# Banded attention units placed between the second pair of forgetting heads' units, their bias table in a raw weight buffer, blocks from the last down

## What is computed

```python
# forgetting attention, head by head, 128 queries at a time
logits = q @ k.T * scale + F[q] - F[k];  causal mask;  p = softmax(logits);  y_f = p @ v
# sliding window of 128, 2 key heads for 4 query heads: a block of 128 queries
# sees 256 keys (its own block and the one before)
logits = q @ band(k).T * scale - slope * dist;  mask dist outside 0..127
p = softmax(concat([logits, sink]))[..., :-1];  y_s = p @ band(v)
```

## Time and profile before

| | us |
|---|---|
| median of 3 runs | 1837.4 (1834.18 to 1841.05) |
| profiled execution | 1835.78 |
| its span on the core | 1834.0 |
| PE busy | 1742.1 (95%) |
| VectorE busy | 888.7 (48%) |
| ScalarE busy | 592.0 (32%) |
| GpSimd busy | 647.1 (35%) |

### The profile page before, as it was taken

The page is one execution under the profiler, slowest core; times in us unless marked ns, Lnnn a source line. Parts: engine busy times, 40 slices in busy tenths (PEclk is TensorE's granted clock), DMA queues, the critical chain, the costliest instruction groups (busy, mean ns, idle before and its releaser), DMA issues.

```text
span 1834.0 us, 22463 instructions
## 1 busy us (share of the span) xinstructions
PE 1742.1 (95%) x8340; PEld 1454.7 (79%) x8340; DVE 888.7 (48%) x1576; ACT 592.0 (32%) x965; POOL 647.1 (35%) x363
## 2 busy tenths in 40 slices
PE   2999999999999999899999979999999999999996
PEld 2887878877888888797887768888888888888885
DVE  5615646469999999275754252221122122022116
ACT  2434234472232222364334473212122112211213
POOL 0521221004356565401884444224214322321424
PEclk9999999998999999999999989999999999999998
DMA  8121131011111111503764212112102111111202
GB/s 302 57 82 45 59 96 39 9 50 32 54 43 54 46 43 63 166 1 137 284 203 161 81 35 69 35 46 65 49 23 69 57 34 46 57 34 46 69 23 92
DMA packets 36292, 135.58 MB, mean 74 GB/s; under 512 B 4496, under 2 KB 4496, under 8 KB 36240
## 3 DMA queue, kind: packets, MB, share of 16 engines
q1 hardware_dynamic: 34000, 127.55, 20.6%
q0 software_dynamic: 2240, 7.34, 1.9%
HBM read 118.62 MB, written 9.96 MB: 70 GB/s over the span
## 4 chain that ended last, share of the span: by engine, by line
PE 89%; DVE 5%; ACT 3%; DMA 2%; issue 1%; POOL 1%; SPq 0%; DVEq 0%; ACTq 0%
PE ps L484 26%; PE ps L486 26%; PE ps L485 26%; PE ps L673 4%; PE ps L652 2%; PE ps L578 1%; PE ps L579 1%; DMA region_b<-in_w_ada 1%; DVE region_a L1569 1%; DVE h_t L1535 1%; ACT y_t L873 1%; ACT region_d L1030 0%; PE ps L684 0%; PE ps L504 0%; DVE region_a L1583 0%
## 5 line engine op out<-in xcount | busy, mean ns | idle before, releaser
L484 PE MATMUL ps<-h_t,w_t 128*128 128x512 f32 x1632 | 640.6, 392 | 6.1 <-POOL w_t L1107 2.4
L485 PE MATMUL ps<-h_t,w_t 128*128 128x512 f32 x1632 | 637.6, 391 | 0.0
L486 PE MATMUL ps<-h_t,w_t 128*128 128x512 f32 x1632 | 637.3, 391 | 0.0
L484 PEld LDWEIGHTS ps<-h_t,w_t 128*128 128x128 f32 x1632 | 308.0, 189 | 73.6 <-issue 4.0
L486 PEld LDWEIGHTS ps<-h_t,w_t 128*128 128x128 f32 x1632 | 307.8, 189 | 64.5
L485 PEld LDWEIGHTS ps<-h_t,w_t 128*128 128x128 f32 x1632 | 308.1, 189 | 64.1 <-issue 0.5
L1107 POOL TENSOR_TENSOR w_t<-raw,w_t 128x1280 fp32r<-128x1280 f32 (+1 forms) x67 | 183.2, 2734 | 251.3 <-ACT w_t L833 161.1
L1578 DVE TENSOR_TENSOR region_d<-ps,region_d 128x512 f32<-128x512 f32 x44 | 30.4, 692 | 439.8 <-PE ps L486 439.8
L1583 DVE TENSOR_TENSOR region_a<-ps,region_a 128x512 f32<-128x512 f32 x176 | 121.1, 691 | 109.5 <-PE ps L486 109.5
L1344 DVE MAX8 top<-region_b 128x8 f32<-128x384 f32 (+5 forms) x192 | 157.9, 882 | 17.3 <-issue 16.7
L1347 DVE MATCH_REPLACE8 region_b<-top,region_b 128x384 f32<-128x384 f32 (+5 forms) x192 | 166.1, 876 | 0.0
(11 more groups left out here) (184 smaller groups left out, 2182.2 us busy)
## 6 DMA issues: line engine op xcount, KB each, us to landing
raw<-in_w_ffn SPq DMA_DIRECT2D x66, 512.0 KB, 3.5
region_b<-in_w_ada SPq DMA_DIRECT2D x48, 512.0 KB, 4.4
raw<-in_w_gates SPq DMA_DIRECT2D x32, 640.0 KB, 3.9
raw<-in_w_z SPq DMA_DIRECT2D x18, 512.0 KB, 3.3
raw<-in_w_o SPq DMA_DIRECT2D x16, 512.0 KB, 3.6
region_a<-in_x SPq DMA_DIRECT2D x8, 512.0 KB, 11.7
mix_dram<-region_a SPq DMA_DIRECT2D x8, 512.0 KB, 6.0
region_a<-mix_dram SPq DMA_DIRECT2D x8, 512.0 KB, 6.6
```

The costliest lines, as they stand in the source:

```text
L484: pe.matmul(o, a_hi, m_hi, start=first, stop=False)
L485: pe.matmul(o, a_hi, m_lo, start=False, stop=False)
L486: return pe.matmul(o, a_lo, m_hi, start=False, stop=last)
```

## The change

The second call of `attention` keeps its 24 units but in another order: after the two forgetting units of block b comes the banded unit of block b+1, and at the very end the banded unit of block 0. So the sequence is f7 f7 f6 f6 s7 f5 f5 s6 f4 f4 s5 f3 f3 s4 f2 f2 s3 f1 f1 s2 f0 f0 s1 s0. A banded block must follow the forgetting block of the same number, since its result overwrites part of the forgetting bias; an assertion says so. Group numbers are now counted from the order of the units. The bias table goes to `raw[:, 1]`, the buffer of tile 17, and tile 17 is loaded after the last unit's reduction. `ya_back` is read back after the last forgetting logits.

```diff
+        def fox_unit_pair(pair, b):
+            return [("fox", b, 2 * pair + j) for j in range(2)]
+
+        first_units = [u for b in reversed(range(TT)) for u in fox_unit_pair(0, b)]
+        second_units = [u for b in reversed(range(TT))
+                        for u in fox_unit_pair(1, b) + ([("swa", b + 1, None)] if b < TT - 1 else [])]
+        second_units.append(("swa", 0, None))
         dsa_units = [("dsa", b, h) for b in reversed(range(TT)) for h in range(HEADS)]
-        units = fox_units + swa_units + dsa_units
+        units = first_units + second_units + dsa_units
+        fox_end = 1 + max(u for u, (kind, b, h) in enumerate(units) if kind == "fox")
+        window_at = raw[:, 1, 0:L]
...
-            for j in range(2):
-                tile_load(T_AFS + j, w_gates[j])
-            sp.wait_ge(s_logit, U_SWA)
-            sp.dma_start(region_d[:, :], window_bias).then_inc(s_table, 16)
-            sp.wait_ge(s_of, O_SWA)
+            tile_load(T_AFS, w_gates[0])
+            sp.wait_ge(s_w_lo, T_AFS)
+            sp.dma_start(window_at, window_bias).then_inc(s_table, 16)
+            sp.wait_ge(s_logit, fox_end)
             sp.wait_ge(s_ya_out, 16 * BT)
             for ch in range(BT):
                 sp.dma_start(ya_back[:, ch], ya_dram[:, ch, :]).then_inc(s_ya_in, 16)
+            sp.wait_ge(s_lg, U_DSA)
+            tile_load(T_AFS + 1, w_gates[1])
...
-                            window_cols(region_d[:, :], b)[:, hh], 1.0, TAKEN, ALU.add, ALU.max,
+                            window_cols(window_at, b)[:, hh], 1.0, TAKEN, ALU.add, ALU.max,
```

More of the change, by code:

```diff
@@ L66 @@
 FFN_AHEAD = ((1,), (2, 3), (4, 5), (6,))
-U_FOX, U_SWA, U_DSA = 0, HEADS * TT, HEADS * TT + TT
-O_FOX, O_SWA, O_DSA = 0, 2 * TT, 3 * TT
+U_FOX, U_DSA = 0, HEADS * TT + TT
+O_DSA = 3 * TT
 MIX0 = 1
@@ L307, in build, with groups_split @@
         act_order = sem("act_order")
-        fox_units = [("fox", b, 2 * pair + j) for pair in range(2) for b in reversed(range(TT)) for j in range(2)]
-        swa_units = [("swa", b, None) for b in range(TT)]
-        dsa_units = [("dsa", b, h) for b in reversed(range(TT)) for h in range(HEADS)]
-        units = fox_units + swa_units + dsa_units
+        def fox_unit_pair(pair, b):
[4 more added lines that the diff above has]
+        second_units.append(("swa", 0, None))
+        dsa_units = [("dsa", b, h) for b in reversed(range(TT)) for h in range(HEADS)]
+        units = first_units + second_units + dsa_units
+        first_swa = min(u for u, (kind, b, h) in enumerate(units) if kind == "swa")
+        fox_end = 1 + max(u for u, (kind, b, h) in enumerate(units) if kind == "fox")
+        window_at = raw[:, 1, 0:L]
+        ends = [kind == "swa" or h in ((1, 3) if kind == "fox" else (HEADS - 1,)) for kind, b, h in units]
+        def groups_split(u):
+            return sum(end and kind != "swa" for end, (kind, b, h) in zip(ends[:u + 1], units))
         def group_of(u):
             kind, b, h = units[u]
[L319 to L323, removed]
+            n = {"fox": 2, "swa": 1, "dsa": HEADS}[kind]
+            j = (h or 0) % n
+            return ends[:u].count(True), j == 0, j == n - 1
         def group_bank(u):
@@ L365, in stack_scale @@
             return HD ** -0.5 if stacks[T][0] == "q" and T >= T_FOX else 1.0
+        assert all(units.index(("swa", b, None)) > units.index(("fox", b, 3)) for b in range(TT))
         def stack_parts(T):
@@ L1448, in group_lo @@
                 else:
-                    dve.wait_ge(s_o_hi, (g if kind == "fox" else g - TT) + 1)
+                    dve.wait_ge(s_o_hi, groups_split(u))
                     dst, src = group_turned(u, y_lo(1))
@@ L1462, in biased @@
                 if kind == "swa":
-                    if u == U_SWA:
+                    if u == first_swa:
                         dve.wait_ge(s_table, 16)
```

## The result

The changed kernel takes 1841.62 us (median of 12 runs, 1836.62 to 1846.3) against 1837.4 us before (12 runs, 1834.06 to 1841.05): ratio 1.0025, 95% interval 1.0014 to 1.0035. The two medians differ by 4.2 us; the ratio says some 4.6 us, with an interval of 2.6 to 6.4 us: slower, clear of noise but inside the half per cent band that the forecast called no change. The forecast was 1842.7 us. Its profiled execution took 1841.77 us, with a span of 1840.0 us (before: 1835.78 and 1834.0).

A forecast was written before the change was run, and what follows sets the result against it. TensorE (PE), busy 95%, was taken as the bound. Idle or lost time goes from 9.6 to 15.8 us (2.9 + 12.9), +6.2, less 0.9 for the gates: net +5.3, median 1842.7 us, range 1833 to 1849 us.

The forecast's parts named there:

- rival A: Tail before the gates keeps full clock, block 1's `den` addition gets in before POOL: +2 us, 1839.4 us; chance 0.20.
- the hole: 2.06 us PE gap where the second pair's banded units start, blamed on the bias table's late DMA.
- The price of 4.7 us: Gain from loading the table early: 2.06 us idle, 1.7 us clock loss and 0.96 us pipeline filling at the banded start.
- Tile 17 and `ya_back`: Their moved loads before the gates cost nothing; tile 17 uncovered would cost up to 4 us.
- The order: In the interleaved units PE waits 0.1, 0.5, 1.05, 1.25 us at blocks 4 to 1: 2.9 us, bounds 0 to 5.
- The tail up to the last transposition: Block 1's banded transposition at 4.8 us, the last at 7.65, with 1.5 and 1.65 us of PE idle.
- time 0: The prediction's mark for the tail: end of the transposition of the second-last forgetting unit (block 0, head 2).
- The clock in the tail: PE falls to half clock at about 7.65 us, making the tail 21.2 us, 12.9 idle or lost, instead of 17.6.
- the second shut-out: In the tail, block 1's `den` addition on DVE misses POOL's start at 11.3 us and waits until 15.8 us.
- The 0.9 us taken off for the gates: Half clock begins earlier, so less of it falls in the gates: 0.9 us, half the difference in loss, subtracted.
- rival C: Clock falls already at the gaps of blocks 2 and 1: +9.5 us, 1846.9 us; chance 0.15.
- B: Rival: gaps at blocks 3 to 1 are filled, tail as before, table gain kept: -4.7 us, 1832.7 us; chance 0.20.

The follow-up runs named there:

- the table alone: Changed kernel with the unit order of before, keeping the table in the raw buffer and the moved loads: 1833.82 us, ratio 0.9982 to the kernel before.
- The shortened exponentials: Changed kernel with one exponential over all four heads of a banded unit in place of four: single execution, 1840.25 us, attention to gates 78.97 us.
- the two repeats: The changed kernel profiled twice more with nothing changed, for its clock: single executions of 1839.25 and 1840.09 us.
- two other orders: Changed kernel with only banded blocks 7 to 4 interleaved (1840.21 us), or with all banded blocks after the forgetting units, 7 down to 0 (1837.12 us, single execution).
- the third execution: The changed kernel, unchanged, profiled a third time: single execution of 1840.09 us, attention to gates 83.10 us.
- the one with the products ahead: Changed kernel with the first 24 gate products issued ahead of the last turning out: 1837.13 us, ratio 0.9998 to the kernel before.

## Why the prediction was right, and where it was not

The way (slightly slower, within half a per cent), the size (+5.3 against +4.6 us) and the main reason held. One step did not, and that the number came out near all the same is in part luck: the tail that was seen is that of rival A (1839.4 us), and some 2 us of the measured time have no shown cause.

**What bounds the kernel, and the hole.** Right. The hole belonged to the table's DMA though the profile named a transposition; the table alone gives 3.1 us. The price of 4.7 us (3.0 of idle time, 1.7 of clock) was too high for the old order: there the table is worth 2.8 us in the trace, 1.8 of them idle time and 1.0 clock. The filling of the banded pipeline, 0.96 us in the earlier trace rows, was counted as gone and became 1.65 us.

**Tile 17 and `ya_back`.** Right: the loads were out at 401.93 and ACT read `ya_back` at 413.78, with no wait. PE has no gap from the start of the gates to 470 us, so the second gate tile did not wait for its weights.

**The order.** Right in mechanism, nearly in size. Forecast gaps for forgetting blocks 4 to 1: 0.1, 0.5, 1.05, 1.25. Measured, with both gaps of a unit added: none at block 4, 0.44 at block 3 (banded block 4), then 0.89 and 1.24. The forecast put each gap whole before the transposition, released by ACT's copy. Half of it or more (0.88 of 1.24) stands before the turning out, released by DVE, whose reductions come before the division in its queue. The shortened exponentials show it: only ACT's share went.

**The tail up to the last transposition.** Forecast 4.8 and 7.65 us after time 0 (404.99 us); measured 4.77 and 7.47. POOL's start: forecast 10.8, measured 10.78. The exclusion: forecast as read from the earlier trace rows, and shown by cutting POOL's instruction (3.03 to 0.63 us).

**The clock in the tail: the step that failed.** "I expect the fall at about 7.65": in the profiled execution it came at 13.3 us, so the values of block 1 ran at full clock, the second shut-out did not happen and the tail was that of case A, 17.6 us forecast, 17.58 measured. The step was not absurd: the kernel with the cut subtraction had the fall at 7.2 us, and the two repeats at 9.2 and 9.3 us (one of them with an earlier fall, 4.4 us ahead of the mark). In all three profiled executions of the changed kernel itself the tail was 17.6 us, in the repeats although half clock ran through part of the values of block 1: the addition got in with 0.28 and 0.34 us to spare. So the forecast 21.2 us was wrong in all three. The long wait of block 1's addition was seen in two other orders (4.12 us each), and there full clock did not prevent it: 0.4 us decided. What was wrong is to give one time for a fall that moved by 4 us, and once came early as well, between executions of the same kernel, and to hang the shut-out on it.

**What met the error.** From attention to gates the forecast's own terms with the tail that was measured give +2.6 us (2.9 + 9.3 idle, less 9.6), and the trace has +2.5: that part is understood. The tail's 3.6 us too much were made up otherwise. The 0.9 us taken off for the gates did not come (half clock lasted 5.9 us in them, as before). The other 2 us of the median are not explained. Half clock sometimes comes already in the new gaps (401.5 us in the third execution, where it cost 1.6 us), which was rival C in small; how often, three executions can't say. The 6.8 us more of half clock near 1097 us explain most of why the two first profiles differ by 6.0 us and not by 2.5, but not the median: the kernel before showed the same stretch in its second profile. Nor was there much more half clock on the whole: the mean granted clock is 0.9837 over the twelve runs of the changed kernel and 0.9841, 0.9838 and 0.9836 over the three sets of 29, 17 and 8 runs of the kernel before, at most some 1.7 us more of half clock or 0.9 us of time, as an estimate from these means. It may fall more often where PE is busy, which these means do not show. And 2.5 us lies only just under the interval of 2.6 to 6.4 us. This stays open.

**Rivals.** B is out: the gaps are there and the table's gain is visible only in the old order. A describes the fixed part. C did not happen as priced; its trigger did, in one of the three profiled executions of the changed kernel, and in that of the one with the products ahead.

## What to carry to other kernels

Mixing two kinds of work in one software pipeline did not help here, since each kind filled PE alone once its pipeline was full; beside the other the long chain of the banded unit (reductions, exponentials, copy) found too little PE work to hide behind, first where the causal blocks were narrow. Before an order is changed, put the chain of each unit against the PE work that lies between its two transpositions, width by width. And at a seam between stages look first for products that need nothing of the stage that ends: here 24 of them moved ahead were worth 4.4 to 7.2 us, more than every reordering.

## What the hardware showed

A small DVE addition of two SBUF operands that is issued while the GpSimd subtraction runs lasts until that subtraction ends: it takes 0.16 us alone, 3.03, 4.12 and 4.12 us here, always to within 0.02 us of POOL's end, and 0.40 and 0.63 us when POOL's instruction is cut in four. Issued 0.28 us before POOL it is not touched.

The Trainium skill ("SBUF — State Buffer", section "Who interferes with whom") states this exclusion, and that the order of issue decides which of the two waits; these rows agree. It sets this tail: issued 0.4 us behind POOL in place of 0.3 to 0.8 us ahead of it, the addition of block 1 makes the way from the last transposition to the gates 13.2 and 13.4 us in place of 10.1.

The granted clock fell to half in the middle of work with gaps of only 0.4 to 1.5 us each, and not at the same place in every execution of the same kernel: 13.3, 9.2 and 9.3 us after time 0 in the three of the changed kernel, and 4.4 us ahead of it as well in one, while the gaps themselves repeat to 0.01 us.
